# Level products of the recurrent heads in pairs, with a second pair of buffers, and a new order on ScalarE and VectorE around them

## The reference, cut to what matters

```python
def step(S, xs):
    qc, kc, gc, vc = xs
    G = jnp.cumsum(gc, axis=-2)
    o_inter = jnp.einsum('bhik,bhkv->bhiv', qc * jnp.exp(G), S)
    diff = G[:, :, :, None, :] - G[:, :, None, :, :]
    decay = jnp.exp(jnp.where(causal[:, :, None], diff, NEG_BIG))
    A = jnp.einsum('bhik,bhijk,bhjk->bhij', qc, decay, kc)
    o_intra = jnp.einsum('bhij,bhjv->bhiv', A, vc)
    G_last = G[:, :, -1:, :]
    S_new = jnp.exp(G_last[:, :, 0, :])[..., None] * S + jnp.einsum(
        'bhjk,bhjv->bhkv', kc * jnp.exp(G_last - G), vc)
    return S_new, o_inter + o_intra
...
h = lax.conv_general_dilated(
    h, cv_w[:, None, :], window_strides=(1,),
    padding=[(CV_WIDTH_FILTER - 1, 0)],
    dimension_numbers=('NWC', 'WIO', 'NWC'),
    feature_group_count=CV_WIDTH) + cv_b
...
mod = c_act @ ada_w[l] + ada_b[l]
sh1, sc1, g1, sh2, sc2, g2 = [m[:, None, :] for m in jnp.split(mod, N_MOD, axis=-1)]
...
mix = jnp.concatenate([o_a, o_b, o_c], axis=-1) @ w_out[l]
x = x + g1 * mix
```

## Time and profile before

| | |
|---|---|
| median of 3 runs | 1178.79 us (1178.68 to 1180.65) |
| profiled execution, its time | 1181.4 us |
| its span in the trace | 1179.6 us |
| mean granted clock of TensorE | 0.997 of full speed |
| TensorE busy | 1167.3 us, 99% |
| VectorE, ScalarE, GpSimd busy | 802.4, 691.1, 455.7 us |

### The profile page before, as it was taken

How to read it: one execution, slowest core, us unless ns; L and a number is a source line. 1 busy time by engine, 2 the same in 40 slices (tenths; PEclk the granted TensorE clock), 3 DMA queues, 4 the chain that set the end, 5 groups by cost and what they waited for, 6 DMA issues and landing times.

```text
span 1179.6 us, 19704 instructions
## 1 busy us (share of the span) xinstructions
PE 1167.3 (99%) x7070; PEld 961.9 (82%) x7070; DVE 802.4 (68%) x1838; ACT 691.1 (59%) x1344; POOL 455.7 (39%) x300
## 2 busy tenths in 40 slices
PE   9999999999999999999999999999999999999998
PEld 8777777778777888789777777779988899899897
DVE  6867777776777877776589766776761375475575
ACT  6766676775436778745467888754431443443542
POOL 0301111112520000053477688315454576666663
PEclk9999999999999999999999999999999999999999
DMA  5523354451534333352322112333463324223322
GB/s 202 164 72 108 91 178 151 154 161 55 195 110 124 94 104 99 117 159 75 110 62 89 37 55 73 125 108 107 142 189 100 106 72 143 81 99 108 108 73 72
DMA packets 41040, 131.82 MB, mean 112 GB/s; under 512 B 4576, under 2 KB 7264, under 8 KB 40944
## 3 DMA queue, kind: packets, MB, share of 16 engines
q1 hardware_dynamic: 35360, 121.39, 32.2%
q10 hardware_dynamic: 5584, 9.18, 2.5%
HBM read 127.10 MB, written 2.13 MB: 110 GB/s over the span
## 4 chain that ended last, share of the span: by engine, by line
PE 88%; issue 4%; POOL 2%; DVE 2%; DMA 2%; ACT 1%; SPq 0%; ACTq 0%; DVEq 0%; POOLq 0%
PE G L1078 18%; PE G L1080 18%; PE G L1079 18%; PE G L2140 2%; PE S L1205 2%; PE G L2142 2%; PE G L2141 2%; PE T L1244 2%; PE O L1265 2%; PE S L1429 1%; POOL wL L642 1%; POOL tmp L680 1%; PE O L1492 1%; PE T L1476 1%; PE S L2140 1%
## 5 line engine op out<-in xcount | busy, mean ns | idle before, releaser
L1078 PE MATMUL G<-hi,wH 128*128 128x512 f32 x1032 | 417.1, 404 | 1.7 <-issue 0.7
L1080 PE MATMUL G<-hi,wL 128*128 128x512 f32 x1032 | 403.6, 391 | 0.0
L1079 PE MATMUL G<-lo,wH 128*128 128x512 f32 x1032 | 403.1, 391 | 0.0
L642 POOL TENSOR_TENSOR wL<-w,wH 128x1024 fp32r<-128x1024 f32 x89 | 219.9, 2476 | 427.5 <-ACT wH L2295 427.4
L1078 PEld LDWEIGHTS G<-hi,wH 128*128 128x128 f32 x1032 | 194.1, 188 | 52.1 <-issue 12.4
L1080 PEld LDWEIGHTS G<-hi,wL 128*128 128x128 f32 x1032 | 194.0, 188 | 41.7
L1079 PEld LDWEIGHTS G<-lo,wH 128*128 128x128 f32 x1032 | 194.4, 188 | 38.6 <-issue 1.9
L2295 ACT ACTIVATE wH<-w 128x1024 fp32r<-128x1024 f32 x140 | 147.3, 1054 | 101.8 <-DMA w<-weights_dram 51.1
L427 POOL TENSOR_TENSOR kd<-kd,band 128x256 f32<-128x256 f32 x8 | 7.2, 901 | 193.1 <-DMA kd<-c_dram 193.1
L2869 DVE TENSOR_TENSOR wL<-w,wH 128x1024 fp32r<-128x1024 f32 x51 | 63.4, 1244 | 16.1 <-ACT wH L2295 16.0
L1195 DVE CUSTOM_DVE_ANT_0 adaw<-adaw,scr 128x1024 f32<-128x1024 f32 x36 | 64.4, 1789 | 0.0
(11 more groups left out here) (565 smaller groups left out, 2542.2 us busy)
## 6 DMA issues: line engine op xcount, KB each, us to landing
w<-weights_dram SPq DMA_DIRECT2D x150, 512.0 KB, 3.6
adaw<-ada_dram SPq DMA_DIRECT2D x48, 512.0 KB, 4.3
wp<-weights_dram SPq DMA_DIRECT2D x20, 512.0 KB, 4.4
kd<-c_dram ACTq DMA_DIRECT2D x16, 512.0 KB, 5.1
xT<-x_dram SPq DMA_DIRECT2D x4, 512.0 KB, 8.1
out_dram<-xT SPq DMA_DIRECT2D x8, 256.0 KB, 2.3
scr<-ca_dram SPq DMA_DIRECT2D x2, 512.0 KB, 6.4
kd<-cbias SPq DMA_DIRECT2D x8, 128.0 KB, 4.0
```

Of the source, the lines that this page charges most:

```text
L642: g.tensor_tensor(wL[:, u.slot], raw_home(u), wH[:, u.slot].bitcast(f32), ALU.subtract).then_inc(w_lo, 1)
L1078: mm(home[:, :], whi, H[:, k, :], start=(k == first), stop=False)
L1079: mm(home[:, :], whi, L[:, k, :], start=False, stop=False)
L1080: last = mm(home[:, :], wlo, H[:, k, :], start=False, stop=(k == final))
```

## The change

**Level products in pairs.** raised(t, n) gives levels 4, 5 and 8 another pair of rows of kd, four rows on. raise_both writes the moved half of the columns from the pair of level n into that of level n+1 (moved_on with two levels). Between levels 3 and 4, 5 and 6, 7 and 8 the pair changes, so the half that does not move has to be copied too: leave(t, n) on ScalarE (left_behind), n = 3, 5, 7, counted by h_moved, for which products 4 and 6, turn_ke and the raise_both behind them wait. raise_both(3), (5) and (7) no longer wait for a product. On TensorE products 3 and 4 stand together, and 5 and 6, and turn_ke stands right behind product 7 instead of at the head of the next window; the gemm pieces between them are put together accordingly.

**ScalarE.** leave is added three times a head. In windows 1 and 2 the exponential of the queries comes before the weight splits, and what was the last pair of filter terms of a window now follows queries of the next one. take_first, take_ke and keys come before take_blocks. CONV_HEAD is 3, 8, 4 for 4, 8, 3 slots. The last window has a function of its own.

**VectorE.** states_of comes before queries_1; raise_both runs ahead of joined in pairs; in the head's normalisation rooted_h, normed_h and gated_h are spread anew; gates(1) comes earlier.

**Modulation.** Behind the last window VectorE works on blocks 0 and 1 only; blocks 2 and 3 follow output unit 1 in add_output. SyncE's queue is the same, word for word.

In the diff the first window(t) is TensorE's, the second ScalarE's (its first half), and the last piece is VectorE's list behind the windows.

```diff
-CONV_HEAD = [4, 8, 3, 0]
+CONV_HEAD = [3, 8, 4, 0]
...
-ADA_PER = {..., "m": (ADA_OM + 4, (0, 0, 0, 1, 1, 0), 48)}
+ADA_PER = {..., "m": (ADA_OM + 2, (0, 2, 0, 1, 1, 0), 48)}
...
-        def raised(t):
-            return kd[:, 2 - 2 * (t % 2), :], kd[:, 3 - 2 * (t % 2), :]
-        def moved_on(t, m):
-            q = raised(t)[0]
+        def raised(t, n):
+            row = 2 - 2 * (t % 2) + (4 if n in (4, 5, 8) else 0)
+            return kd[:, row, :], kd[:, row + 1, :]
+        def moved_on(t, m, n):
+            q = raised(t, n)[0]
             return bass.AP(q.tensor, q.offset + m, [list(q.ap[0]), [SEQ - m, 2], [2 * m, SEQ // (2 * m)], [1, m]])
+        def left_behind(t, m, n):
+            q = raised(t, n)[0]
+            return bass.AP(q.tensor, q.offset, [list(q.ap[0]), [SEQ + m, 2], [2 * m, SEQ // (2 * m)], [1, m]])
...
             def product(t, p):
                 pe.wait_ge(sem("h_x"), 8 * t + max(p, 1) + since("h_x"))
+                if p in (4, 6):
+                    pe.wait_ge(*mark("h_moved", 3 * t + p // 2 - 1))
...
             def window(t):
                 opened(t)
                 fill(t, 3)
+                fill(t, 4, (0, 1))
                 product(t, 3)
+                product(t, 4)
                 if t == 2:
                     conv_sum()
-                fill(t, 4)
-                product(t, 4)
+                fill(t, 4, (2, 3))
                 fill(t, 5)
                 product(t, 5)
+                product(t, 6)
                 if t == 2:
                     conv_sqsum()
                 fill(t, 6)
-                product(t, 6)
                 fill(t, 7, (0, 1))
                 product(t, 7)
+                turn_ke(t)
                 fill(t, 7, (2, 3))
...
+            def leave(t, n):
+                m = 1 << (n - 1)
+                act.wait_ge(sem("h_x"), 8 * t + n + since("h_x"))
+                if n == 3 and t > 1:
+                    act.wait_ge(sem("h_o"), t - 1 + since("h_o"))
+                s.activation(left_behind(t, m, n + 1), left_behind(t, m, n), ACT.Copy).then_inc(sem("h_moved"), 1)
...
             def window(t):
-                take_ke(t - 1)
                 queries(t)
-                if t == 1:
-                    split_h(5)
-                split_h(4 * t + 2)
+                conv_terms(t - 1, 2 if t == 1 else 7)
                 silu_scalar_2(act, "hq", t, kraw[:, :])
-                conv_terms(t, 0)
+                split_h(4 * t + 1)
+                split_h(4 * t + 2)
                 raw_h(t, 2, vraw, sem("h_vturn"), t + since("h_vturn"))
+                conv_terms(t, 0)
+                square_h(t - 1)
                 conv_terms(t, 1)
-                square_h(t - 1)
                 conv_terms(t, 2)
+                leave(t, 3)
...
             def raise_both(t, n):
                 m = 1 << (n - 1)
-                dve.wait_ge(sem("h_products"), 8 * t + (2 if n == 1 else n + 1) + since("h_products"))
+                if n in (1, 2, 4, 6):
+                    dve.wait_ge(sem("h_products"), 8 * t + (2 if n == 1 else n + 1) + since("h_products"))
+                if n in (4, 6):
+                    dve.wait_ge(*mark("h_moved", 3 * t + n // 2 - 1))
...
-                v.tensor_tensor(moved_on(t, m), moved_on(t, m), by, ALU.mult).then_inc(sem("h_x"), 1)
+                v.tensor_tensor(moved_on(t, m, n + 1), moved_on(t, m, n), by, ALU.mult).then_inc(sem("h_x"), 1)
...
+            last_window()
+            states_of(3)
             silu_z(3)
             blocks(0, 1)
-            states_of(3)
             silu_vector_2(dve, "h", 3, zraw[:, :], zsig, mark("h_gated", 3))
-            blocks(1, 4)
+            blocks(1, 2)
```

204 lines of the change are left out of this document (120 added, 84 removed).

## The result

| | before | changed |
|---|---|---|
| median, us | 1180.33 (1178.68 to 1181.59) | 1191.51 (1191.08 to 1192.61) |
| profiled execution, span | 1179.6 | 1189.7 (1191.5 in all) |
| its granted clock, mean | 0.997 | 0.993 |

The account below looks back on a forecast made before the run. TensorE, busy 99% of the span, was taken as the bound, with losses where helpers or loads come late. Terms +0.75 (conv_sum), -1.25 (work behind it) and +4.0 (tail) gave +3.5 on 1178.79: 1182.3 us, range 1175.8 to 1186.3.

Parts of the forecast that it names:

- Pairs: TensorE's level products in four windows: 0.34 us saved for each of eight pairs, 2.7 us; 3.2 us with product 7's new neighbours.
- Product 7 and the transposes as neighbours: On TensorE, four times: worth between 0 and 0.34 us each, taken as 0.12, 0.5 us in all.
- conv_sum: Window 2: GpSimd's last filter addition ends near 739.6, TensorE stops about 3 us; net term +0.75 us.
- Everything that windows 0 to 2 gained: At conv_sum in window 2: earlier gains and small stops vanish because the chain over ScalarE and GpSimd sets the time.
- 0.3 early: Window 1: ScalarE enters the stretch ahead of queries(2) about 0.3 us earlier, so queries(2) start near 720.5.
- some 0.9 late: Product 6 in window 1: ScalarE's copy comes near 710, some 0.9 us late, a small stop swallowed later.
- The stop of 0.48 ahead of product 0: Window 1: TensorE's stop of 0.48 us can go, since keys and powers come earlier.
- In windows 0 and 3 I find ScalarE in time: Windows 0 and 3: ScalarE is in time for all its added copies and the products behind them; no loss counted.
- The tail: Ahead of the last two output units: unit 6's load 5.2 us later behind blocks 2 and 3; term +4.0 us.
- The rivals: Four other outcomes for the whole kernel: 1178.3 (chance 0.14), 1180.0 (0.14), 1176.0 (0.19), and 1183.3 or 1184.3 us (0.07).
- the faster one: Both conv_sum's chain and the tail's block chain are hidden: -2.8 us, 1176.0 us, chance 0.19.

Follow-up runs that it names:

- (9): Changed kernel with GpSimd's filter additions of windows 1 and 2 on 128 columns in place of 500: 1184.9 us, ratio 1.0052.
- (2): Changed kernel with VectorE's root of the state norm moved behind raising level 4 and joining product 3, in windows 1 and 2: 1191.7 us.
- (5): Changed kernel with VectorE's root behind joining product 4 and ScalarE's second leave copy right behind its own root: 1191.3 us.
- (15): Changed kernel with GpSimd's two weight subtractions at the start of window 3 on one eighth of the columns: 1187.6 us, ratio 1.0070.
- (8): Kernel before with only the modulation change, blocks 2 and 3 behind the sum of output unit 1: 1183.1 us, ratio 1.0034.
- (1): Changed kernel with only the modulation change undone, blocks 2 and 3 back ahead of the first output sum: 1197.1 us, ratio 1.0143.
- (16): Changed kernel with ScalarE's weight splits, and the pair of filter terms between queries and splits, back where the kernel before has them: 1183.0 us, ratio 1.0046.
- 17: Changed kernel with ScalarE's weight splits and modulation blocks 2 and 3 both back in their old places: 1184.1 us, ratio 1.0035.
- (2 to 6): Five versions of the changed kernel, each mending one stop by reordering VectorE or ScalarE or moving a filter pair: 1191.7, 1192.9, 1191.7, 1191.3, 1191.4 us.
- (11): Changed kernel with the order edits for single stops, filter pairs 4, 8, 3 and output units 6 and 7 loaded earlier, all together: 1186.1 us, ratio 1.0050.
- 12: Kernel before with chains of 5, 8 and 12 one-column matmuls, each waiting for the last, ahead of three sums of squares: 1194.9 us.
- (7): Changed kernel with output units 6 and 7 loaded ahead of modulation blocks 4 and 5 in SyncE's list: 1189.5 us, ratio 1.0078.

## Why the prediction was wrong, point by point

**Pairs: right.** The row of the changed kernel that answers to the earlier trace rows has 0.32, 0.51, 0.57 and 0.34 again:

```profile
700.60 0.39 PE L1087 MATMUL G<-hi,wL 128*128 128x512 f32 x1
700.92 0.69 PE L1926 MATMUL T<-kd 128*64 128x64 f32 x16
701.43 0.64 PE L1926 MATMUL S<-kd 128*64 128x64 f32 x16
702.00 0.50 PE L1085 MATMUL G<-hi,wH 128*128 128x512 f32 x1
702.34 0.39 PE L1086 MATMUL G<-lo,wH 128*128 128x512 f32 x1
```

With GpSimd out of the way (9) TensorE won 2.6 us over windows 0 to 2, and over all windows its own work is 3.7 shorter, 0.5 more than forecast. Product 7 and the transposes as neighbours are worth 0.06 in windows 1 and 2 (from the last wide matmul ahead of product 7 to the second behind the transposes, less 0.23 for each wide matmul: 1.15 apart, 1.09 together), half of the 0.12 that I took. The copies took 0.62.

**conv_sum: mechanism and size right, its use wrong.** Halves behind ScalarE's later splits, eight additions behind them, a stop:

```profile
725.21 5.18 POOL L649 TENSOR_TENSOR wL<-w,wH 128x1024 fp32r<-128x1024 f32 x2 [1.19 <-ACT wH L2304]
...
738.21 1.26 POOL L687 TENSOR_TENSOR tmp<-tmp,sq 128x511 f32<-128x511 f32 x1
```

The stop was 2.17, forecast 3. The step that failed is "Everything that windows 0 to 2 gained, the stop of 0.48 and any small stop at product 6 in window 1 included, is swallowed here". Two things make the chain late. ScalarE does not enter this stretch 0.3 early but late, and the change also puts VectorE's states_of ahead of queries_1, so that a wait for TensorE gets into a chain that I had let run on ScalarE and GpSimd alone. VectorE waits for TensorE's products for the state, ScalarE for VectorE's step of the queries, and the splits stand behind that. ScalarE's root of the norm, before and changed; then the start of queries(2) and what follows it:

```profile
703.75 0.68 ACT L783 ACTIVATE rinv<-N,epsc 128x512 f32<-128x512 f32 x1
...
702.01 0.68 ACT L790 ACTIVATE rinv<-N,epsc 128x512 f32<-128x512 f32 x1
...
718.87 0.60 ACT L1093 ACTIVATE kraw<-G 128x512 f32<-128x512 f32 x1
...
721.86 0.29 DVE L3279 COPY scr<-T 128x128 f32<-128x128 f32 x1 [1.77 <-PE T L1951]
...
723.55 0.63 ACT L1104 ACTIVATE kraw<-kraw 128x512 f32<-128x512 f32 x1 [1.54 <-DVE kraw L1099]
724.09 1.99 ACT L2304 ACTIVATE wH<-w 128x1024 fp32r<-128x1024 f32 x2
```

To compare with the kernel before, add the 3.6 us by which this trace is early at matmul 3700. The root comes 1.9 late (705.6). Queries(2) start 2.0 behind my forecast (722.5 for 720.5), the wait for VectorE adds 1.5, and the halves begin at 728.8 where I had put 725.3. TensorE lost 4.1 us in window 1 to stops and low clock, and the chain was late by nearly as much, so the loss was not swallowed: the stop at conv_sum came on top. How much of it travelled by which wait is read from the rows; no run puts queries_1 first again.

**Window 1: mis-sized.** What I had put at "some 0.9 late" was 1.97 + 0.26 + 0.16 at products 5 and 6. I had reckoned ScalarE's copy only, and on a ScalarE that would come earlier; in fact it waits 3.8 us between 693 and 702 for freed term buffers, since GpSimd adds behind later halves. VectorE's root, put ahead of level 4, waits for the same ScalarE. The two causes were equally late (2), and the z rows a third (5). The stop of 0.48 ahead of product 0, which I had put as gone, became 0.96.

**Window 3: missed.** "In windows 0 and 3 I find ScalarE in time" was an answer to the wrong question. The later splits put GpSimd's halves beside VectorE's silu and scaling, and TensorE stood 2.0 us (15). I used that very effect, for the tail alone.

**The tail: right.** The rows that answer to the earlier trace rows:

```profile
795.86 14.97 SPq L485 DMA_DIRECT2D adaw<-ada_dram  x4
810.87 0.91 SPq L480 DMA_DIRECT2D w<-weights_dram  x2
...
804.69 2.43 DVE L1202 CUSTOM_DVE_ANT_0 adaw<-adaw,scr 128x1024 f32<-128x1024 f32 x1
...
807.07 3.40 DVE L1202 CUSTOM_DVE_ANT_0 adaw<-adaw,scr 128x1024 f32<-128x1024 f32 x1
...
815.49 1.06 ACT L2304 ACTIVATE wH<-w 128x1024 fp32r<-128x1024 f32 x1 [9.98 <-DMA w<-weights_dram]
```

The load goes out at 810.87; 801.13 plus the 4.6 that TensorE is late by then is 805.7: 5.2 late, as forecast. The stop is 3.53 for +4.0, and 3.40 with this part alone (8). What I did not see is that the alternative was worse in the changed kernel (1).

**The clock: missed.** No term of the sum had it: 6.8 us, the largest error. This is the term that I put at nothing without a reason. The profile of before shows it once, behind a stop of 0.9 us near 320 us, and I had not asked what a stop does beyond its own length.

**The sum.** Forecast +3.5; add 2.4 (window 1), 2.0 (window 3) and 6.8 (clock), take off 0.8 and 0.5 for the two stops that were shorter: 13.4, against 13.8 in the traces. By part, the later splits, with the pair of terms ahead of them, cost 8.5 us (16) and the blocks' move 4.4 by itself (8). That VectorE's order makes the rest of the tail's loss is argued from the rows of 17; no run undoes it. The rivals: none came true; the faster one had the right price for the pairs and missed the same stops.

## What to carry to other kernels

A part of a change can be priced only beside the others: the blocks' move cost 4.4 us alone and saved 5.6 with the rest in place, and mends of one stop (2 to 6) only handed TensorE to the next chain, which was as late. All of them together (11) gave 5.4 us. Look for what the late chains have in common (here ScalarE's splits, which start GpSimd's halves, which hold VectorE and SyncE's loads) and undo that. And count the clock: in these traces a stop of 2 us mostly cost 1.7 us more than its length.

## What the runs showed of the hardware

In the stretch from 640 to 830 us the profiled executions of the changed kernel and of all experiments but 12 have 48 stops of TensorE between 1.89 and 6.26 us; at 39 of them a stretch of 3.4 us (6.8 in six cases) at 1.2 GHz began between the start of the stop and 1.5 us behind its end. Of 26 stops between 0.85 and 1.63 us none had one. The length of a stop does not settle it alone. Near 320 us all twenty traces have some 2 us of one-column matmuls. Five have a stop of 0.78 to 0.91 us ahead of them, and in all five the clock fell 1.3 to 3.0 us after the stop's end; of the other fifteen, with no stop over 0.3 us there, it fell in one (7). And the same stop can go without (2.18 us at conv_sum in 1 and 7), so one kernel's times spread: (16) took 1181.97 us with a mean clock of 0.997 and 1186.80 with 0.994. The Trainium skill (TensorE: Matmul & The Clock Gate, "What's actually happening") has the gate choose between two levels by how busy the array has been; the records here agree on the two levels, they hold 1.0 and 0.5 and nothing else.
